# A two-layer network on one core: second attention by two heads and two query blocks, rings of PSUM banks, and three smaller moves

## What is computed

```
first block:   h = rms_norm(x); (conv parts, q, k, v, iq, ik, iw, gates) = h @ w_in
               y_a = conv(...) @ w_branch_a
               scores iq.ik choose 256 keys per query (a mask for each query block)
               attn: 8 heads of 64 share one k, v; softmax over the chosen keys + T5 bias
               x += (gate_a * y_a + gate_b * (attn @ w_branch_b)) @ w_out; then a gated FFN
second block:  a pooling mixer, then one K and V for 2 groups of heads (64 channels each):
  q, z = split(h @ w_in);  q *= 1/8                      # 16 heads, 8 share a K/V group
  for each block of 128 queries n, head g:               # keys: block n-1 and block n
    s = q[n,g] @ kb[n].T + pos_bias[g];  s = where(band, s, NEG)
    m = max(s.max(), sink[g]);  p = exp(s - m)
    p = p / (p.sum() + exp(sink[g] - m));  o[n,g] = p @ vb[n]
  x += gate * ((o * silu(z)) @ w_out)
```

## Time and profile before

| | |
|---|---|
| median of 3 runs | 2679.21 us (2678.14 to 2681.87) |
| the profiled execution, its own time | 2682.51 us |
| its span in the trace | 2680.7 us |
| mean granted clock of PE, share of full speed | 0.972 |
| PE busy with matmuls | 2530.8 us, 94% |
| DVE / ACT / POOL busy | 1707.4 / 970.6 / 632.2 us |
| second attention on the time axis | about 2417 to 2575 us |

### The profile page before, as it was taken

How to read it: one execution, slowest core, us unless ns; L and a number is a source line. 1 busy time by engine, 2 the same in 40 slices (tenths; PEclk the granted TensorE clock), 3 DMA queues, 4 the chain that set the end, 5 groups by cost and what they waited for, 6 DMA issues and landing times.

```text
span 2680.7 us, 31860 instructions
## 1 busy us (share of the span) xinstructions
PE 2530.8 (94%) x12136; PEld 2089.1 (78%) x12136; DVE 1707.4 (64%) x2896; ACT 970.6 (36%) x1749; POOL 632.2 (24%) x473
## 2 busy tenths in 40 slices
PE   5899999888999899999999999999999989999898
PEld 3778888677787688888888877888877767788887
DVE  5499999477424887876644367567676564008843
ACT  4431212477223332222312243233242244227742
POOL 2147522476543000000000220000000144323343
PEclk7999999899999999999999998999999998999899
DMA  4112233100454256654623132232264114331143
GB/s 166 44 30 72 80 94 95 52 1 9 155 180 145 88 187 184 193 173 150 226 75 116 63 95 79 102 103 84 98 259 150 56 55 155 97 103 60 52 150 102
DMA packets 260706, 293.17 MB, mean 109 GB/s; under 512 B 10856, under 2 KB 216140, under 8 KB 260556
## 3 DMA queue, kind: packets, MB, share of 16 engines
q1 hardware_dynamic: 260556, 291.14, 33.5%
HBM read 223.95 MB, written 66.10 MB: 108 GB/s over the span
## 4 chain that ended last, share of the span: by engine, by line
PE 66%; DVE 26%; ACT 5%; issue 1%; DMA 1%; POOL 1%; SPq 0%; DVEq 0%; ACTq 0%; POOLq 0%
PE ps L67 64%; DVE sm L100 6%; DVE m L97 6%; DVE tmp L103 2%; ACT tmp L73 2%; DVE tmp L79 2%; DVE sm L79 2%; PE ps L70 1%; DVE p2l L76 1%; DVE tmp L76 1%; ACT pth L73 1%; DVE X L79 1%; DVE pwa L76 1%; DVE wl L76 1%; DVE B2l L76 1%
## 5 line engine op out<-in xcount | busy, mean ns | idle before, releaser
L76 POOL TENSOR_TENSOR wl<-raw,wh 128x512 fp32r<-128x512 f32 (+1 forms) x224 | 292.1, 1325 | 1620.0 <-ACT wh L73 1619.7
L73 ACT ACTIVATE wh<-raw 128x512 fp32r<-128x512 f32 (+1 forms) x388 | 226.4, 621 | 244.7 <-PE ps L67 186.2
L73 ACT ACTIVATE tmp<-ps 128x512 f32<-128x512 f32 (+5 forms) x172 | 127.3, 751 | 392.5 <-PE ps L67 380.0
L67 PE MATMUL ps<-B2h,wh 128*128 128x512 f32 x616 | 244.8, 397 | 12.3 <-DVE B2l L76 6.8
L67 PE MATMUL ps<-B2h,wl 128*128 128x512 f32 x616 | 242.3, 393 | 0.0
L67 PE MATMUL ps<-B2l,wh 128*128 128x512 f32 x616 | 241.9, 393 | 0.0
L76 DVE TENSOR_TENSOR tmp<-tmp,ps 128x512 f32<-128x512 f32 x204 | 138.4, 685 | 108.7 <-PE ps L67 93.7
L67 PE MATMUL ps<-ah,wh 128*128 128x512 f32 (+1 forms) x608 | 192.5, 393 | 14.3 <-DVE xt L85 10.3
L73 ACT ACTIVATE wh<-ws 128x512 fp32r<-128x512 f32 x152 | 94.4, 626 | 292.3 <-DVE ws L76 265.4
L67 PE MATMUL ps<-B3h,wh 128*128 128x512 f32 x448 | 180.5, 403 | 14.7 <-DVE B3l L76 7.4
L67 PE MATMUL ps<-al,wh 128*128 128x512 f32 (+1 forms) x608 | 191.2, 391 | 0.0
(11 more groups left out here) (282 smaller groups left out, 5845.9 us busy)
## 6 DMA issues: line engine op xcount, KB each, us to landing
ada<-in_ada_w SPq DMA_DIRECT2D x48, 512.0 KB, 3.8
raw<-in_w_in SPq DMA_DIRECT2D x37, 512.0 KB, 4.4
raw<-in_a_w_in SPq DMA_DIRECT2D x33, 512.0 KB, 4.5
gates<-tmp SPq DMA_DIRECT2D x32, 512.0 KB, 3.0
raw<-in_w_ffn_gate SPq DMA_DIRECT2D x24, 512.0 KB, 6.4
hd<-tmp SPq DMA_DIRECT2D x22, 512.0 KB, 4.5
gf<-hd SPq DMA_DIRECT2D x22, 512.0 KB, 7.3
raw<-in_a_w_out SPq DMA_DIRECT2D x20, 512.0 KB, 3.5
```

The source lines that it names most:

```text
L67: return self.e.matmul(*a, **k) if self.e else Ins()
L73: return self.e.activation(*a, **k) if self.e else Ins()
L76: return self.e.tensor_tensor(*a, **k) if self.e else Ins()
```

## The change

Second attention. The keys of both groups get tiles of their own (`K2`), 128 rows filled by one copy and one subtraction; the V of both groups lie in one strip `vc` (and a last block `vend`) in which a block of 64 columns of V stands between blocks of zeros, so that an even or odd head's view is a shift by 64 columns. All of them are made among the projections. An item is now a pair of heads by two query blocks. Its scores are 12 products on 64 rows, one head's in rows 0 to 63 and the other's in 64 to 127, into two halves. The halves go in rings: four for scores, three for turns, one for outputs. The maximum is taken negated, which drops the negation; the sink's difference is made on POOL (`sink`), `o2l` moves from DVE to POOL, and copies and subtractions of the turned probabilities go by halves. The values of an item are 18 products (12 where block 0 is in it).

First attention's keys: both halves of `kt2` are filled by DMA, so one ACT copy and one subtraction do; the second set's subtraction moves from DVE to POOL.

Branch: the copies `ch` move into the end of ACT's attention, and DVE takes two of the four `cl`.

```diff
@@ first attention's keys (SP, ACT, and DVE or POOL)
+        e.dma_start(self.kt2[0:64, :], self.kt[0:64, :]).then_inc(self.sig["swap0"].up(("first", 0)), 16)
         e.dma_start(self.kt2[64:128, :], self.kt[0:64, :]).then_inc(self.sig["swap0"].up(("swap", 0)), 16)
...
+        e.activation(self.KH[:, :], self.kt2[:, :], ACT.Copy).then_inc(self.sig["ahi"].up(("khi", i)), 1)
+
+    def k_lo(self, e, i, signal):
+        e.wait_ge(*self.at("khi", i))
+        e.tensor_tensor(self.KL[:, :], self.kt2[:, :], self.KH[:, :].bitcast(F32), ALU.subtract).then_inc(
+            signal.up(("klo", i)), 1)
...
     def dve_qkv(self, e):
-        self.dve_k_lo(e, 1)
...
     def pool_qkv(self, e):
         self.pool_w(e, "kv")
+        self.k_lo(e, 1, self.sig["plo"])
@@ branch: ACT's attention, then DVE and POOL
+        def conv(n):
+            if n < 63:
+                return
+            e.wait_ge(*self.at("top", 63))
+            for j in range(4):
+                e.wait_ge(*self.at("chl", j))
+                e.activation(self.ch[j][:, :], self.tmp[(self.CH + j) % 5][:, :], ACT.Copy).then_inc(
+                    self.sig["ahi"].up(("chi", j)), 1)
-        pipeline(64, [(4, turned), (2, norm), (7, stored), (0, exps)])
+        pipeline(64, [(4, turned), (2, norm), (7, stored), (0, exps), (4, conv)])
...
     def dve_branch(self, e):
+        e.wait_ge(*self.at("pv", 31))
+        for j in range(2):
+            self.conv_lo(e, j, self.sig["vlo"])
...
     def pool_branch(self, e):
+        for j in range(2, 4):
+            self.conv_lo(e, j, self.sig["plo"])
@@ second attention, PE
+    ITEMS2 = [(j, m) for j in range(8) for m in range(4)]
...
+            ps = [self.take(e, ("s2", n, odd), ring=self.p_score) for odd in (0, 1)]
+            for i in range(2):
+                blk = 2 * m + i
...
+                for t, (q, kk) in enumerate(((QH, KH), (QH, KL), (QL, KH))):
+                    for p, r in zip(ps, (slice(0, 64), slice(64, 128))):
+                        ins = e.matmul(p[:, o:i * 256 + 256], q[r, c], kk[r, k], start=t == 0, stop=t == 2)
...
+            if m % 2 == 0:
+                self.take(e, ("o2", n // 2), ring=self.p_out)
...
+                for blk, c0, c1, p0 in ((2 * m, 0, 256, 128), (2 * m + 1, 128, 256, 384), (2 * m - 1, 0, 128, 0)):
...
-        self.part_banks()
-        pipeline(32, [(4, other_values), (0, lambda n: score(n) if n != 16 else None), (3, turn), (4, values),
-                      (0, lambda n: score(n) if n == 16 else None)])
-        self.join_banks()
+        tiles = sorted(self.pool4, key=lambda i: max(x.taken for x in self.halves[2 * i:2 * i + 2]))
+        h = [self.halves[2 * i + k] for i in tiles for k in (0, 1)]
+        self.p_score, self.p_turn, self.p_out = h[0:4], h[4:7], h[7:8]
+        pipeline(32, [(0, score), (3, turn), (4, values)])
@@ second attention, ACT, DVE and POOL
-        pipeline(32, [(4, other_values), (0, other_keys), (3, turned), (5, stored), (-2, begin), (0, exps)])
+        pipeline(32, [(3, turned), (5, stored), (-2, begin), (0, exps)])
...
-            ins.then_inc(vec.up(("most2", n), ("free", ("s2", n))), 1)
-            e.wait_ge(*self.at("most2", n))
-            e.tensor_scalar(nm, mm, -1.0, None, ALU.mult).then_inc(vec.up(("top2", n)), 1)
...
-        pipeline(32, [(4, other_values), (0, other_keys), (2, norm), (0, top), (5, stored), (3, turned_low),
-                      (5, stored_low), (-2, begin)])
+        pipeline(32, [(2, norm), (0, top), (5, stored), (3, turned_low), (-2, begin)])
...
+        pipeline(32, [(0, sink), (2, norm), (5, stored_low)])
```

More of the change, by code:

```diff
@@ new lines, in turn @@
+            for odd in (0, 1):
+                p = self.take(e, ("p2", n, odd), ring=self.p_turn)
+                for i in range(4):
+                    ins = e.transpose(p[:, i * 128:i * 128 + 128], L[:, odd * 512 + i * 128:odd * 512 + i * 128 + 128],
+                                      self.ident[:, :])
+                ins.then_inc(self.sig["prod"].up(("prod", ("p2", n, odd)), *([("l2free", n)] if odd else [])), 1)
+        def values(n):
+            j, m = self.ITEMS2[n]
+            if m % 2 == 0:
+                self.take(e, ("o2", n // 2), ring=self.p_out)
+            po, (PH, PL) = self.ps(("o2", n // 2)), self.pt2[n % 2]
+            e.wait_ge(*self.at("v2lo", j // 4))
+            c = m % 2 * 256
+            for odd in (0, 1):
+                e.wait_ge(*self.at("p2lo", n, odd))
+                for blk, c0, c1, p0 in ((2 * m, 0, 256, 128), (2 * m + 1, 128, 256, 384), (2 * m - 1, 0, 128, 0)):
+                    if blk < 0:
+                        continue
+                    V, pc = [self.v2(j // 4, low, blk, odd) for low in (0, 1)], slice(odd * 512 + p0, odd * 512 + p0 + c1 - c0)
+                    ins = self.prods(e, po[:, c + c0:c + c1], V, (PH[:, pc], PL[:, pc]),
+                                     m % 2 == 0 and odd == 0 and blk == 2 * m, m % 2 == 1 and odd == 1 and blk == 2 * m - 1)
@@ L2925, in exps @@
         def exps(n):
-            j, hb, odd = self.ITEMS2[n]
             L = self.tmp[n % 4]
-            mm, nm, sm, es, rd = self.st2(n)
-            sk = self.sk[:, 2 * j + odd:2 * j + odd + 1]
-            e.wait_ge(*self.at("top2", n))
-            for i in range(4):
-                o = i * 256 + (128 if hb == 0 and i == 0 else 0)
-                e.activation(L[:, o:i * 256 + 256], L[:, o:i * 256 + 256], ACT.Exp, bias=nm[:, i:i + 1],
-                             accum_out=sm[:, i:i + 1])
@@ L2935, in exps @@
-            e.activation(es, nm, ACT.Exp, bias=sk).then_inc(self.sig["evac"].up(("exp2", n)), 1)
+            mm, sm, es, rd = self.st2(n)
+            for odd, i, k, o in self.each2(n):
+                e.wait_ge(*self.at("top2", n, odd))
+                o += 256 * k
+                e.activation(L[:, o:k * 256 + 256], L[:, o:k * 256 + 256], ACT.Exp, bias=mm[:, k:k + 1], scale=-1.0,
+                             accum_out=sm[:, k:k + 1])
+            e.wait_ge(*self.at("sink2", n))
+            e.activation(es, es, ACT.Exp).then_inc(self.sig["evac"].up(("exp2", n)), 1)
```

265 lines of the change are left out of this document (124 added, 141 removed).

## The result

The changed kernel takes 2684.84 us (median, 2682.02 to 2687.76), the kernel before 2677.62 beside it (2674.74 to 2681.87): the ratio is 1.0026, 95% interval 1.0016 to 1.0035, about 7 us slower. Forecast were 2666.5 us and a range of 2644 to 2682; the time lies above both, in the case that had a chance of 0.09.

The account below looks back on a forecast made before the run. The prediction took the chain as two thirds PE and a quarter DVE, with DVE setting the second attention's steady items. Window -3.3, keys -3.9 and branch -5.5 gave -12.7, 2666.5 us on the median's scale; range 2644 to 2682.

Parts of the forecast that it names:

- the case that had a chance of 0.09: Whole kernel: the changed kernel measures slower than the kernel before; chance 0.09.
- Keys and table, -3.9: First attention: earlier keys' subtraction on POOL ends PE's wait for the bias table and its slow flips; -3.9 us.
- Branch, -5.5: Branch stage: early copies and DVE's share of `cl` let PE start sooner and reach `oh` earlier; -5.5 us.
- rival D: The two early gains are eaten by the next late input and don't reach the end; 2675 us, chance 0.14.
- Window, -3.3: Second attention: slower items +8.6, middle -10.9, filling and draining -1; together -3.3 us.
- The wait for the output half, 1.2 to 1.65 in each second item: Second attention: PE's values stall until DVE empties the one output half; 4.62 us an item instead of 4.29.
- POOL's sink sum, "I take 0.2": Second attention: POOL's new four-column sum, ahead of its product in the queue, priced at 0.2 us.
- DVE 3.6 us an item: Second attention: DVE's work per item falls from 4.29 to 3.6 us.
- rival C: Second attention: PE's clock falls in the stalls, 3 us more per affected item; 2705 us if half are, chance 0.08.
- Filling and draining, -1 (-3 to +2): Ends of the second attention: draining 1 to 2 us shorter, filling as now; -1 us taken.
- The middle, -10.9: Second attention's middle: the second group's keys and values move among the last projections, saving 10.9 us.
- Rival B: Second attention: the output bank doesn't bind, the busiest engine sets 3.85 us an item; 2646 us, chance 0.20.

Follow-up runs that it names:

- early_only: Kernel before with only the first attention's keys and the branch parts of the change, second attention as it was; 2669.2 us, ratio 0.9970 to before.
- stored_first: Changed kernel with DVE's multiplication of the output bank put ahead of the four maxima of its step; 2676.9 us, ratio 0.9994 to before.
- out_two: Changed kernel with two PSUM halves for the second attention's output and two, not three, for turned probabilities; 2674.5 us, ratio 0.9989 to before.
- product_first: Changed kernel with POOL's product of item n - 2 ahead of its sink sum for item n; 2673.0 us, ratio 0.9977 to before.
- product_twice: Changed kernel with product_first's swap and turns_twice's repeated transposes, one output half kept; 2669.1 us, ratio 0.9960 to before.
- turns_twice: Changed kernel with the last four transposes of every odd turn done three times, output unchanged; 2676.7 us, ratio 0.9992 to before.
- two_product: Changed kernel with two output halves and POOL's product ahead of its sink sum; 2651.9 us, ratio 0.9897 to before.
- two_parts_product: Changed kernel with two output halves, queries' subtraction in two halves on DVE, and POOL's product ahead of its sink sum; 2651.2 us, ratio 0.9893 to before.
- two_parts: Changed kernel with two output halves and the queries' subtraction on DVE in two halves; 2659.4 us, ratio 0.9929 to before.
- window_only: Kernel before with only the second attention's part of the change; 2697.8 us, ratio 1.0071 to before.

## Why the prediction was wrong, point by point

**Keys and table, -3.9: right.** From the trace 518.26 - 513.35 = 4.9, of which 0.8 was there before the stage began, so 4.1; alone 2.7 with an interval that holds it. The second DMA and POOL's `kp` cost nothing, and no `wl` came late.

**Branch, -5.5: right.** From the attention's last product to the first `oh` product 20.05 us became 15.0; alone 4.9. DVE's `ol` took 10.89 beside POOL's `cl`, as the earlier trace rows had said.

**That both reach the end (against rival D): right**, 8.8 of 9.4. In the one profile of the changed kernel 3.8 us of it seemed to be lost in the first attention, where PE ran at the low clock for longer after the start. From 520 to 540, the changed kernel:

```profile
520.00:540.00 20.00, 17.82 (x106) 13.07 (x104) 12.35 (x70) 15.00 (x57) 10.04 (x14) 0.64 0.01 2
```

and early_only, with the same instructions up to there:

```profile
520.00:540.00 20.00, 17.16 (x104) 12.70 (x102) 12.33 (x68) 15.26 (x59) 10.28 (x14) 0.68 0.01 2
```

From 540 to 560 the clock is 0.91 in the one and 1.00 in the other, from 640 to 676 it is 0.95 and 1.00. Four kernels whose instructions are the same up to the branch (the changed one, early_only, stored_first, out_two) have the first `ch` product at 676.42, 673.18, 673.38 and 672.95. So 3 us of it were of one execution, and a reading of one pair of traces would have blamed the change for them.

**Window, -3.3: wrong, +12.6 in the trace and +15.6 by medians.** In parts, from the trace:

- *The wait for the output half, 1.2 to 1.65 in each second item: right*, 1.1 to 1.5, twelve times. An item at 4.62 by it: 4.57 once the next term is out.
- *POOL's sink sum, "I take 0.2": this is the step that failed first.* The instruction does take 0.20. But I priced its duration and not its wait. It waits for the maxima of item n, and behind it in POOL's queue stands the product of item n - 2, ready 1.9 us before. My own rule, to name what is queued behind an added wait, was used for SP's load and PE's values and not here; the text even has it "ahead of the 1.89 us product in POOL's queue". Cost: 0.8 us of PE's wait in four items, 2.0 of the filling, and the next point's first half; 11.8 by medians, with all that hangs on it.
- *DVE 3.6 us an item: mis-sized, 4.4.* It is busy 17.58 us in the four items from 2459.07 to 2478.18. The new meeting of DVE's and POOL's work on SBUF was not in the sum. DVE's addition of four columns takes 0.67 in the mean (0.15 before) and `q2l` 2.20 (1.22 before). Groups from 2430 to 2560, after:

```profile
L76 DVE TENSOR_TENSOR st<-st 128x4 f32<-128x4 f32 x26 | 17.4, 670 | 0.0
...
L76 DVE TENSOR_TENSOR q2l<-tmp,q2h 128x1024 fp32r<-128x1024 f32 x6 | 13.2, 2198 | 2.7 <-ACT q2h L73 2.7
```

  The 0.34 us an item that `o2l` freed on DVE came back as 0.25 of `q2l` (0.98 in four items) and 0.52 of addition; 3.6 and these two make the 4.4. What they cost apart from the sum's place in the queue no run shows. I used this effect in the branch, from the earlier trace rows, and left it out where the change itself sets it up. The Trainium skill states it, in SBUF — State Buffer, SBUF: two separate sides: an operation of VectorE with two inputs in SBUF and one of GpSimd that reads SBUF lock each other out for a whole instruction. The trace agrees: the addition begun at 2472.45 ends at 2473.48, the product at 2473.45. `p2l`, with one input in PSUM, stays at 0.68 beside the same product.
- *The low clock (rival C, 0.08): came true, 8.6 us.* My ground against it was that the gap of 1.2 to 1.65 lay under those after which the trace of before showed a fall (1.99). The length of one gap did not tell: here gaps of 1.39, 0.83 and 1.15 us lie within eleven us (up to 2486.14), and the transposes behind them, at 2489.98, take 1.97 us instead of 1.09. The first attention, with PE's waits of 1.1 to 1.5, 9 to 14 us apart, kept its clock in the trace of before (in that of the changed kernel it fell there too, at 667); product_first, with waits of 1.2 to 1.5 each 9 to 12 us and none for POOL, did not (0.93 from 2430 to 2560). What sets the two apart no run shows, so the one was no ground for a chance of 0.08. What the Trainium skill tells in TensorE: Matmul & The Clock Gate, A second HAM failure mode: psum-queue depth-cycling, is what this trace shows; I had it, and gave the word to a row of another stage.
- *Filling and draining, -1 (-3 to +2): +0.9, inside its range.* To the score of item 6 it is 21.0 us instead of 20.3, and from the score of item 31 to the end of the window 17.9 instead of 17.7. The one was forecast as unchanged, the other 1 to 2 us shorter. With the sum behind the product and the gaps filled (product_twice) the two ends take 37.1 us instead of 38.0, the forecast's -1.
- *The middle, -10.9: right.* There is no hole between items 12 and 18 beyond the pattern and the clock.

Check of the sum: the items 6 to 31 take 115.5 in the forecast, 5.1 more by the pattern of 19.1 (25 intervals of 4.82 in turns_twice) and 8.6 by the clock, 129.1 measured; before, 117.4 (the forecast had 25 x 4.29 + 10.9 = 118.2). With the 0.9 of both ends the window is 12.6 longer.

**Rival B** (the bank never binds, 2646, 3.85 us an item) is what two_product and two_parts_product come near to with two output halves and the swap: 2651.9 and 2651.2, 4.0 us an item. The gain was in the change's design. One half of PSUM and one place in a queue kept it away. These two kernels are faster than the kernel before by 1.0% and 1.1%.

## What to carry to other kernels

An instruction that is added to an in-order queue holds all that stands behind it for as long as it waits for its own input, whatever its duration: ask for each added instruction when its input is there and whether work that is ready already stands behind it, and put the ready work first. Waits of 1.1 to 1.5 us that come every nine or ten us on PE are to be priced with the low clock behind them, also where each is shorter than a gap after which it fell before. The shares of the chain are of the whole span: before they are read for one stage, look at the chain in that stage. And when an edit gains nothing or loses, try it again once the tighter limit is gone: the queries in halves lost 4 us at one output half and gained 15 at two.

## What the runs showed of the hardware

- A DVE addition of 128x4 took 0.15 us alone (0.14 to 0.16 in the kernel before) and up to 1.03 beside POOL's 1.89 us product of `tmp` in SBUF, ending with it; a 128x1024 subtraction took 2.20 instead of 1.22 beside POOL's `o2l` of 1.28.
- With PE's waits at 1.1 to 1.5 us, twice in nineteen, and a third of 0.8, the granted clock from 2430 to 2560 was 0.92; with transposes in the longer ones (0.25 to 0.5 left of each, the 0.8 as it was) it was 1.00, and the kernel 8.2 us faster for 128 instructions more. In two_parts, where the only waits are for POOL's product, 0.6 and 1.0 to 1.4 by turns, it was 1.00 too. In window_only and the changed kernel it fell at the same items.
- At the start of the first attention the length of the slow stretch differs between executions of the same instructions by up to 3.5 us: 676.42 and 672.95 at the first `ch` product.
